# A transformer layer in split fp32: the first-stage modulation spread in eight pieces through the first head pair

## The chip, the cores and the metric

One Trainium2 chip, one core of it. The metric is the time of one execution on the device in microseconds (us), and the median over runs is what two kernels are compared by.

## What is computed

One layer of a diffusion-like transformer for 256 latent tokens `x`, with 256 context tokens `ctx` beside them, width 2048, 16 heads of 128:

```python
s_lat = silu(c); s_ctx = silu(c_ctx)                 # 2048 each
m_lat = split(s_lat @ w_ada + b_ada, 6)              # shift, scale, gate | shift, scale, gate
m_ctx = split(s_ctx @ w_ada + b_ada, 6)              # only shift and scale are used
a_lat = modulate(rms_norm(x, norm_mix), m_lat[0], m_lat[1])
a_ctx = modulate(rms_norm(ctx, norm_mix), m_ctx[0], m_ctx[1])
y = hgrn2_mixer(a_ctx, a_lat, ...)                   # w_in, w_f, gated linear scan per head, w_o
h = x + m_lat[2] * y
h = h + m_lat[5] * swiglu(modulate(rms_norm(h, norm_ffn), m_lat[3], m_lat[4]))
out = rms_norm(h, final_norm)
```

Everything is fp32. `w_ada` is 2048 x 12288 fp32; its first 4096 columns (shift and scale of the mixer, 32 MB) are needed for both token sets, the other 8192 for the latent tokens alone.

## The kernel before, in words

**Numbers.** TensorE multiplies in a rounded format (fp32r). Each weight chunk of 128 x 1024 floats is loaded into a ring of four slots (`raw`), ScalarE (ACT) writes its rounded part (`whi`, `hi`, L484) and VectorE (DVE) the rest (`wlo`, `lo`, L807), both in rings of three. Activations are split likewise into `ahi` and `alo`. A product is three matmuls. A matmul in plain fp32 is two records in the trace.

**Stage 1, the modulation.** 64 blocks of `w_ada` (128 rows x 1024 columns) are taken in four quarters of the columns, 16 blocks each. silu(c) and silu(c_ctx) stand in TensorE as four columns and the weights move, 512 columns at a time. 40 blocks are split (L1244, L1246), 24 go unsplit in fp32 through six slots of their own, `dslot` (L1236). The sums are four rows, which ACT copies (L502) and TensorE turns (L1256) before DVE makes `mod`, `modc` and `scl` of them. The 64 transposes of `x` and `ctx` (L1274) lie behind block 6, the matmul that spreads the mean squares (L1290) behind block 8. ACT modulates (L525), rounds (L528) and DVE makes the rest (L842).

**Stage 2, eight head pairs.** Each pair has 16 chunks: eight VQ (values and queries, 36 matmuls of 256 columns, the `v_bank` ones at L1310 to L1312) and then eight Z (both forget gates, 24 matmuls of 512 columns, L1295 to L1297). The scans of heads whose pairs are done run in steps between the chunks, by a table written by hand. DVE meanwhile adds up the other 96 blocks of `w_ada` (six sums that end by chunk 150, `ADA_ENDS`, one DVE operation of L903 for each block, then eight fp32 matmuls with one column, L1529).

**Stage 3, the output gate.** 32 chunks of `w_in`, here called the gate stage, with the scans of the last heads beside them.

**Stage 4 to 6.** Projection with `w_o` (32 chunks, `wide`, L1439 to L1441), FFN gate and up (176 chunks, L1419 to L1421), down (88 chunks, `wide` again). In the projection, SyncE (SP) asks for chunk 0, then waits for the last head's scan and asks for `x` by token, the gate row and the final weight (3.5 MB), then for chunk 1. ACT evacuates the last output gates (`gate_silu(3)`) before it splits chunk 1. The last three chunks of down run bank by bank (`wide_end`), so that the closing work can begin on the first bank.

The order on every engine is written by hand: each engine runs its own list in order, and semaphores tie the lists.

Of the kernel before, what the change touches and what calls it, by code (L numbers as in the profile page):

```python
# [19 lines left out]
F32 = mybir.dt.float32  # L20
# [30 lines left out]
def ada_direct(k):  # L51

    return k % 8 in (1, 4, 6)


SPLIT_ADA = [c for c in range(4 * KD) if not ada_direct(c % KD)]
DIRECT_ADA = [c for c in range(4 * KD) if ada_direct(c % KD)]
DIRECT = 6


def ada_column(q):

    return (2 * (1 - q % 2) + q // 2) * CW


X_AT = 6
C_B = len(SPLIT_ADA)
# [33 lines left out]
def positions():  # L101


    for g in range(GROUPS):
        for p in range(BODY):
            kind = "Z" if p % 16 >= 8 else "VQ"
            tasks = [(j, 4 * g + off) for j, off in tasks_at(p) if 4 * g + off >= 0]
            yield C_B + g * BODY + p, kind, 2 * g + p // 16, p % 8, tasks
    for p in range(32):
        yield C_G + p, "G", p // 8, p % 8, tasks_tail(p)  # L110


def build(nc, x, c, ctx, c_ctx, w_ada, b_ada, norm_mix, norm_ffn, lb_logits, w_in, w_f, o_norm, w_o,
# [4 lines left out]
    wada = w_ada[0].rearrange("(k p) n -> k p n", p=P)  # L118
    win = w_in[0].rearrange("(k p) n -> p k n", p=P)
# [6 lines left out]
    with stack:  # L126
# [61 lines left out]
        cs4 = sb("cs4", [P, KD, 2, 2], F32R)  # L188
        csd = sb("csd", [P, KD, 2, 2])
        xsum = sb("xsum", [P, 4])  # L190
        mod = sb("mod", [P, 6, KD])
        modc = sb("modc", [P, 2, KD])
        arow = aacc[0:4, :]
        scl = sb("scl", [P, 2, KD])
# [30 lines left out]
        s_c4 = sem("silu_c_split")  # L225
        s_ar = sem("mod_rows_ready")
        s_at = sem("mod_rows_turned")
# [9 lines left out]
        s_mod = sem("mod_steps")  # L237
# [81 lines left out]
        def _(sp):  # L319
# [19 lines left out]
            def load(ck):  # L339
# [3 lines left out]
                if ck < C_B:  # L343

                    q, k = divmod(SPLIT_ADA[ck], KD)
                    col = ada_column(q)
                    whole(slot, dst, wada[k, :, col:col + CW])
                elif ck < C_G:
                    pr, r = divmod(ck - C_B, 16)
                    kk = 2 * (r % 8)  # L350
# [22 lines left out]
            def load_direct(j):  # L373
                if j >= DIRECT:
                    sp.wait_ge(s_du, j - DIRECT + 1)
                q, k = divmod(DIRECT_ADA[j], KD)
                col = ada_column(q)
                sp.dma_start(dslot[j % DIRECT], wada[k, :, col:col + CW]).then_inc(s_dir[j % DIRECT], 16)

            for rb in range(4 * KD):  # L380
                if rb == 2:
                    sp.dma_start(brow[0:96, :], b_ada[0].rearrange("(k p) -> k p", p=P)).then_inc(s_vrow, 16)
                    sp.dma_start(vrow[R_ONORM:R_ONORM + 1, :], o_norm).then_inc(s_vrow, 16)
                if rb == X_AT:
                    for t in range(4):
                        sp.dma_start(xin[:, t, :], crows[t] if t < 2 else xrows[t - 2]).then_inc(s_x[t], 16)
                if ada_direct(rb % KD):
                    load_direct(DIRECT_ADA.index(rb))
                else:
                    load(SPLIT_ADA.index(rb))  # L390

# [16 lines left out]
            for ck in range(C_B, CHUNKS):  # L408
                load(ck)
                if ck == C_B + 4:  # L410
                    sp.dma_start(keep[:, :], keep_in).then_inc(s_keep, 16)
                    sp.dma_start(masks[:, :], masks_in).then_inc(s_keep, 16)
# [44 lines left out]
        def abank(q, i):  # L457

            return (score[0:4, i, :] if q % 2 == 0 else (bank[3], ob)[i][0:4, :])
# [18 lines left out]
        def _(act):  # L478
# [12 lines left out]
            for i in range(2):  # L491
                act.activation(cs[:, :, i], mx[:, 224 + i * KD:224 + (i + 1) * KD], ACT.Silu).then_inc(s_cs, 1)
            act.wait_ge(s_cs, 2)
            act.activation(cs4[:, :, :, 0], cs[:, :, :], ACT.Copy).then_inc(s_c4, 1)

            def mod_rows(q):

                act.wait_ge(s_used, C_B // 4 * (q + 1))
                if q:
                    act.wait_ge(s_at, q)  # L500
                for i in range(2):
                    act.activation(arow[:, i * 512:(i + 1) * 512], abank(q, i), ACT.Copy).then_inc(s_ar, 1)  # L502

            def x_rstd():

                for t in range(4):
# [12 lines left out]
            def modulate(k):  # L519

                act.wait_ge(s_mod, 6 if k < 8 else 11)
                act.wait_ge(s_xn, k + 1)
                for i in range(2):
                    v = xn[:, k, i * T:(i + 1) * T]
                    act.activation(v, v, ACT.Identity, bias=(modc, mod)[i][:, 0, k:k + 1],  # L525
                                   scale=scl[:, i, k:k + 1]).then_inc(s_am, 1)
# [3 lines left out]
            for rb in range(4 * KD):  # L530
                if rb == X_AT:
                    x_rstd()
                if not ada_direct(rb % KD):
                    hi(SPLIT_ADA.index(rb))
                if rb == 5:
                    act.preload_act_table_set(EXP_LN)
                if rb == 11:
                    act.wait_ge(s_lb, 1)
                    act.activation(lbt[:, 1, :], lbt[:, 0, :], ACT.Exp).then_inc(s_lb, 1)
                if rb == 10:  # L540
                    act.wait_ge(s_ms, 1)
                    act.activation(rstd[:, :], bank[2][:, :], ACT.Copy).then_inc(s_rs, 1)
                if rb % KD == 2 and rb > KD:
                    mod_rows(rb // KD - 1)
                if 40 <= rb < 56 and rb % 2 == 0:
                    modulate(rb // 2 - 20)
            hi(C_B)
            mod_rows(3)
            hi(C_B + 1)
            for k in range(8, KD):  # L550
                modulate(k)
                if k % 2 == 1:
                    hi(C_B + k // 2 - 2)
            for i in range(6, KD // 2 + 2):
                hi(C_B + i)

# [33 lines left out]
            def queries(pr):  # L590
                b = pr % 2
                act.wait_ge(s_used, C_B + 16 * pr + 8)
# [66 lines left out]
            for ck, kind, u, r, tasks in positions():  # L659
                if ck > C_B + KD // 2:  # L660
                    hi(ck + 1)
                if kind == "Z" and r == 0:
# [11 lines left out]
                if kind == "Z" and r == 0:  # L674
# [18 lines left out]
            for k in range(KD):  # L693
# [5 lines left out]
                else:  # L699
# [74 lines left out]
            for i in range(2 * KF):  # L774
# [5 lines left out]
                if i == 0:  # L780
# [23 lines left out]
        def _(dve):  # L804
# [6 lines left out]
            dve.memset(csd[:, :, :, 1], 0.0)  # L811
            dve.memset(eps[:, :], EPS).then_inc(s_one, 1)
            dve.wait_ge(s_cs, 2)
            dve.tensor_copy(csd[:, :, :, 0], cs[:, :, :]).then_inc(s_c4, 1)
            dve.wait_ge(s_c4, 2)
            dve.tensor_tensor(cs4[:, :, :, 1], cs[:, :, :], cs4[:, :, :, 0].bitcast(F32), ALU.subtract).then_inc(s_c4, 1)
            am = mx[:, 0:128].rearrange("p (m k s i) -> p m k s i", m=2, s=2, i=2)

            def modulation(q):


                m, half = 1 - q % 2, q // 2
                ks = slice(8 * half, 8 * half + 8)
                b = bias[:, m * KD + 8 * half:m * KD + 8 * half + 8]
                first = 2 + 5 * half + 3 * (q % 2)
                dve.wait_ge(s_at, q + 1)
                dve.tensor_tensor(mod[:, m, ks], am[:, q % 2, ks, 0, 0], b, ALU.add)
                dve.tensor_tensor(modc[:, m, ks], am[:, q % 2, ks, 1, 0], b, ALU.add).then_inc(s_mod, 1)
                dve.wait_ge(s_mod, first)
                dve.tensor_tensor(mod[:, m, ks], am[:, q % 2, ks, 0, 1], mod[:, m, ks], ALU.add)  # L830
                dve.tensor_tensor(modc[:, m, ks], am[:, q % 2, ks, 1, 1], modc[:, m, ks], ALU.add).then_inc(s_mod, 1)
                if m == 1:
                    dve.wait_ge(s_mod, first + 1)
                    nm = vec[:, R_NMIX + 8 * half:R_NMIX + 8 * half + 8]
                    dve.scalar_tensor_tensor(out=scl[:, 0, ks], in0=modc[:, 1, ks], scalar=1.0, in1=nm, op0=ALU.add,
                                             op1=ALU.mult)
                    dve.scalar_tensor_tensor(out=scl[:, 1, ks], in0=mod[:, 1, ks], scalar=1.0, in1=nm, op0=ALU.add,
                                             op1=ALU.mult).then_inc(s_mod, 1)
# [5 lines left out]
            for rb in range(4 * KD):  # L844
                if rb == X_AT:
                    dve.wait_ge(s_vecT, 1)
                    dve.tensor_copy(vec[:, :], mx[:, 0:VROWS]).then_inc(s_vec, 1)
# [815 lines left out]
```

## Time and profile before

| | |
|---|---|
| median of 3 runs | 1844.18 us (1842.5 to 1844.32) |
| the profiled execution | 1842.78 us, span in the trace 1841.0 us |
| TensorE (PE) busy | 1782.6 us, 97% |
| weight loads (PEld) busy | 1500.8 us, 82% |
| DVE busy | 1264.4 us, 69% |
| ACT busy | 899.4 us, 49% |
| chain that ended last | PE 84%, DVE 10%, issue 2%, ACT 2%, DMA 2% |
| mean granted TensorE clock | 0.992 |

The profile is one execution. Busy times of an engine are a union over its instructions; matmuls overlap, so the distance from one start to the next is what a matmul costs in a stream, not its own length. The chain of waits goes back from the last instruction to what released each. Stretches are given in us from the span's start: stage 1 is 0 to 112, the first pair 112 to 191, pairs two to eight 191 to 843, the gate stage 843 to 983, the projection 983 to 1086, gate and up to 1580, down to the end.

### The profile page before, as it was taken

To read this page: it belongs to the slowest core of one execution; us is meant where nothing else is said; L and a number is where in the kernel's file an instruction comes from. 1 tells how busy PE (TensorE), PEld (TensorE's weight loads), DVE (VectorE), ACT (ScalarE), POOL (GpSimd) and SP (SyncE) were. 2 spreads that over 40 slices of the span, in tenths; PEclk is the share of its full clock that TensorE was granted. 3 is DMA by queue.
4 is the path that set the end of the run, shared out by engine and by line. 5 is a ranking of instruction groups with operands and counts; after the bars stand their busy time and mean duration, and the time that the engine had idled before them with its cause. 6 is when DMAs were issued, how large, how long until landed. Compare 5 with 4: busy or idle time off the path is not lost.

```text
span 1841.0 us, 25084 instructions
## 1 busy us (share of the span) xinstructions
PE 1782.6 (97%) x9791; PEld 1500.8 (82%) x9791; DVE 1264.4 (69%) x1977; ACT 899.4 (49%) x1279; POOL 0.2 (0%) x4
## 2 busy tenths in 40 slices
PE   7999999999999999999888989999999999999997
PEld 2268989898989898988787878888888888788885
DVE  6763779796979796979975575555555555555755
ACT  6673535354545454545454554444444444455554
POOL 0000000000000000000000000000000000000000
PEclk9999999999999999999999999999999999999998
DMA  9974544554444554444656556777767776655553
GB/s 357 370 232 157 183 144 142 162 159 139 140 147 149 159 165 135 149 138 139 225 185 230 174 164 204 242 225 229 233 214 224 237 221 216 204 193 194 192 193 121
DMA packets 178136, 353.82 MB, mean 192 GB/s; under 512 B 16929, under 2 KB 82786, under 8 KB 176994
## 3 DMA queue, kind: packets, MB, share of 16 engines
q1 hardware_dynamic: 177826, 352.18, 59.4%
q8 instruction: 77, 1.26, 0.3%
q14 instruction: 41, 0.34, 0.1%
q10 hardware_dynamic: 192, 0.05, 0.0%
HBM read 350.06 MB, written 2.11 MB: 191 GB/s over the span
## 4 chain that ended last, share of the span: by engine, by line
PE 84%; DVE 10%; issue 2%; ACT 2%; DMA 2%; ACTq 0%; DVEq 0%
PE bank L1419 9%; PE bank L1421 9%; PE bank L1420 9%; PE bank L1295 8%; PE bank L1296 7%; PE bank L1297 7%; PE bank L1310 3%; PE bank L1439 3%; PE bank L1311 3%; PE bank L1440 3%; PE bank L1312 3%; PE bank L1441 3%; PE score L1499 2%; DVE wlo L807 2%; DVE aacc L903 2%
## 5 line engine op out<-in xcount | busy, mean ns | idle before, releaser
L807 DVE TENSOR_TENSOR wlo<-raw,whi 128x1024 fp32r<-128x1024 f32 x496 | 605.3, 1223 | 442.7 <-ACT whi L484 442.0
L484 ACT ACTIVATE whi<-raw 128x1024 fp32r<-128x1024 f32 x496 | 523.0, 1058 | 671.4 <-PE bank L1421 227.0
L1295 PE MATMUL bank<-ahi,whi 128*128 128x256 f32 (+1 forms) x1024 | 352.4, 344 | 10.8 <-DVE wlo L807 10.5
L1296 PE MATMUL bank<-alo,whi 128*128 128x256 f32 (+1 forms) x1024 | 344.8, 337 | 0.0
L1297 PE MATMUL bank<-ahi,wlo 128*128 128x256 f32 (+1 forms) x1024 | 344.7, 337 | 0.0
L1419 PE MATMUL bank<-whi,ahi 128*128 128x512 f32 x704 | 275.9, 392 | 1.8 <-DVE alo L1138 1.8
L1421 PE MATMUL bank<-whi,alo 128*128 128x512 f32 x704 | 274.5, 390 | 0.0
L1420 PE MATMUL bank<-wlo,ahi 128*128 128x512 f32 x704 | 274.4, 390 | 0.0
L1295 PEld LDWEIGHTS bank<-ahi,whi 128*128 128x128 f32 x1024 | 194.7, 190 | 32.2 <-DVE wlo L807 10.2
L1297 PEld LDWEIGHTS bank<-ahi,wlo 128*128 128x128 f32 x1024 | 194.7, 190 | 20.3
L1296 PEld LDWEIGHTS bank<-alo,whi 128*128 128x128 f32 x1024 | 194.9, 190 | 19.0
L1419 PEld LDWEIGHTS bank<-whi,ahi 128*128 128x128 f32 x704 | 132.6, 188 | 29.4 <-issue 2.2
L1421 PEld LDWEIGHTS bank<-whi,alo 128*128 128x128 f32 x704 | 132.4, 188 | 27.8
L1420 PEld LDWEIGHTS bank<-wlo,ahi 128*128 128x128 f32 x704 | 132.7, 188 | 27.1
L903 DVE SCALAR_TENSOR_TENSOR aacc<-raw,cs,aacc 128x1024 f32<-128x1024 f32 x120 | 153.5, 1279 | 0.5
L1310 PE MATMUL bank<-whi,ahi 128*128 128x256 f32 x512 | 147.3, 288 | 1.3 <-DVE arena L916 1.2
L1312 PE MATMUL bank<-whi,alo 128*128 128x256 f32 x512 | 144.8, 283 | 0.0
L1311 PE MATMUL bank<-wlo,ahi 128*128 128x256 f32 x512 | 144.7, 283 | 0.0
L1439 PE MATMUL bank<-whi,ahi 128*128 128x512 f32 x240 | 94.9, 396 | 8.9 <-DVE wlo L807 8.9
L1310 PEld LDWEIGHTS bank<-whi,ahi 128*128 128x128 f32 x512 | 98.1, 192 | 2.7 <-DVE wlo L807 2.5
L1311 PEld LDWEIGHTS bank<-wlo,ahi 128*128 128x128 f32 x512 | 98.1, 192 | 0.2
L1312 PEld LDWEIGHTS bank<-whi,alo 128*128 128x128 f32 x512 | 98.0, 191 | 0.0
(226 smaller groups left out, 2285.5 us busy)
## 6 DMA issues: line engine op xcount, KB each, us to landing
raw<-in_w_ada_dram SPq DMA_DIRECT2D x168, 512.0 KB, 3.9
raw<-in_ffn_w_gate_dram SPq DMA_DIRECT2D x88, 512.0 KB, 3.9
raw<-in_ffn_w_up_dram SPq DMA_DIRECT2D x88, 512.0 KB, 4.1
raw<-in_ffn_w_down_dram SPq DMA_DIRECT2D x88, 512.0 KB, 4.2
raw<-in_hg_w_in_dram SPq DMA_DIRECT2D x128, 256.0 KB, 3.4
raw<-in_hg_w_f_dram SPq DMA_DIRECT2D x128, 256.0 KB, 3.5
raw<-in_hg_w_in_dram SPq DMA_DIRECT2D x32, 512.0 KB, 4.6
raw<-in_hg_w_o_dram SPq DMA_DIRECT2D x32, 512.0 KB, 4.1
```

What stands on the lines that cost most here:

```text
L484: act.activation(whi[:, ck % SPL, :], raw[:, q % RAW, :], ACT.Copy).then_inc(s_hi, 1)
L807: dve.tensor_tensor(wlo[:, ck % SPL, :], raw[:, SEQ["w", ck] % RAW, :], whi[:, ck % SPL, :].bitcast(F32), ALU.subtract).then_inc(s_lo, 1)
L903: dve.scalar_tensor_tensor(out=aacc[:, :], in0=block, scalar=cs[:, k, 0:1], in1=aacc[:, :], op0=ALU.mult, op1=ALU.add).then_inc(s_ac, 1)
L1295: pe.matmul(dst, w, ah, start=start, stop=False, skip_group_check=True)
L1296: pe.matmul(dst, w, al, start=False, stop=False, skip_group_check=True)
L1297: return pe.matmul(dst, wl, ah, start=False, stop=stop, skip_group_check=True)
L1310: pe.matmul(dst, ahi[:, k, tk], whi[:, s, o], start=st, stop=False, skip_group_check=True)
L1311: pe.matmul(dst, ahi[:, k, tk], wlo[:, s, o], start=False, stop=False, skip_group_check=True)
L1312: last = pe.matmul(dst, alo[:, k, tk], whi[:, s, o], start=False, stop=end, skip_group_check=True)
L1419: pe.matmul(dst, ahi[:, k, tk], whi[:, s, o], start=first, stop=False)
L1420: pe.matmul(dst, ahi[:, k, tk], wlo[:, s, o], start=False, stop=False)
L1421: last = pe.matmul(dst, alo[:, k, tk], whi[:, s, o], start=False, stop=end)
```

## The change

- Stage 1 no longer stands ahead of the mixer. The 64 blocks are cut anew: eight pieces of 256 channels, eight blocks each, a block being 2 x 128 rows of 256 shift and 256 scale columns (two DMAs of 256 KB with 1 KB rows, `load_mod`). The weights stand in fp32, unsplit, and silu(c), silu(c_ctx) move as two columns: eight matmuls for each block (`mod_block`), through the six slots of `dslot`. The sums come out as columns, so nothing is copied and turned; one DVE pair (`modulation(e)`) gives shift and scale of a piece.
- Twelve blocks run ahead of chunk 0, the other 52 run four to a chunk between the parts of chunks 0 to 12. Chunks of the first pair alternate VQ, Z, and the first pair's Z sums lie in other banks.
- `x` and `ctx` are loaded first and turned ahead of the first block. The rows of vectors (`vrow`, `brow`) are turned before them.
- The ends of DVE's six sums move from (34, 54, 82, 102, 131, 150) to (22, 50, 70, 98, 118, 150).
- Projection: SP asks for chunks 0 to 4 before it waits for the last scan; ACT splits chunk 1 before `gate_silu(3)`. Down: `turn_hidden` and what surrounds it lie behind chunk 1, not 0; `wide_end` takes two chunks, not three; the closing DVE operations are in another order.

```diff
-            for rb in range(4 * KD):
-                if rb == 2:
-                    sp.dma_start(brow[0:96, :], b_ada[0].rearrange("(k p) -> k p", p=P)).then_inc(s_vrow, 16)
...
+            def load_mod(n):
+
+                if n >= DIRECT:
+                    sp.wait_ge(s_du, n - DIRECT + 1)
+                e, j = divmod(n, 8)
+                for m in range(2):
+                    sp.dma_start(dslot[n % DIRECT][:, m * 512:(m + 1) * 512].rearrange("p (k n) -> p k n", k=2),
+                                 wmod[:, 2 * j:2 * j + 2, m * D + e * 256:m * D + (e + 1) * 256]).then_inc(s_dir[n % DIRECT], 16)
+
+            for t in range(4):
+                sp.dma_start(xin[:, t, :], crows[t] if t < 2 else xrows[t - 2]).then_inc(s_x[t], 16)
+            sp.dma_start(brow[0:96, :], b_ada[0].rearrange("(k p) -> k p", p=P)).then_inc(s_vrow, 16)
+            sp.dma_start(vrow[R_ONORM:R_ONORM + 1, :], o_norm).then_inc(s_vrow, 16)
+            for n in range(8):
+                load_mod(n)
...
             for ck in range(C_B, CHUNKS):
+                if ck == 1:
+                    for n in range(8, FIRST):
+                        load_mod(n)
+                elif ck >= 2:
+                    for n in mod_blocks(ck - 2):
+                        load_mod(n)
                 load(ck)
...
-                if ck == C_WO:
+                if ck == C_WO + 4:
 
                     sp.wait_ge(s_on, HEADS)
...
+        def mod_block(pe, n):
+
+            e, j = divmod(n, 8)
+            pe.wait_ge(s_dir[n % DIRECT], 32 * (n // DIRECT + 1))
+            if n == 0:
+                pe.wait_ge(s_cs, 2)
+            if j == 0 and e >= 2:
+                pe.wait_ge(s_md, 2 * e - 1)
+            w = dslot[n % DIRECT].rearrange("p (s k n) -> p s k n", k=2, s=2)
+            for k in range(2):
+                for i in range(4):
+                    last = pe.matmul(mod_sums(e)[:, 2 * i:2 * i + 2], w[:, i // 2, k, i % 2 * P:(i % 2 + 1) * P], cs[:, 2 * j + k, :],
+                                     start=(n in (0, 8) and k == 0 and i == 0), stop=(j == 7 and k == 1), skip_group_check=True)
+            last.then_inc(s_du, 1)
...
+            pe.wait_ge(s_vrow, 16 * 6)
+            pe.transpose(score[:, 1, 0:VROWS], vrow[0:VROWS, :], ident[0:VROWS, 0:VROWS])
...
+            for i in range(KD):
+                turn_x(i)
+            for n in range(FIRST):
+                mod_block(pe, n)
+                if n == 3:
...
+                    if u == 0 and i < 4:
+                        for n in mod_blocks(ck)[i:i + 1]:
+                            mod_block(pe, n)
...
-            wide_end([(C_DN + i, i % YR) for i in range(2 * KF - 3, 2 * KF)], s_db)
-
-
-ADA_ENDS = (34, 54, 82, 102, 131, 150)
+            wide_end([(C_DN + i, i % YR) for i in range(2 * KF - 2, 2 * KF)], s_db)
+
+
+ADA_ENDS = (22, 50, 70, 98, 118, 150)
```

PE at the start of the program, as it was: `mx` and `score` are sums, `cs` and `csd` silu(c) standing, `work` and `arena` hold `dslot` and `x`.

```order
L1264 MATMUL mx<-ident,crow 128x32
L1244 MATMUL score<-whi,cs 4x512
L1246 MATMUL score<-wlo,cs 4x512
...
L1236 MATMUL score<-work,csd 4x512 x2
...
L1281 MATMUL mx<-ident,arena 128x65
L1282 MATMUL mx<-ident,arena 128x96
L1274 MATMUL bank<-ident,arena 128x128 x64
```

PE at the same place in the changed kernel, up to the first part of chunk 0 (L1189 is `mod_block`, 8 rows to a block; `ob` and `mx` its sums; L1242 to L1244 `v_bank`):

```order
L1198 MATMUL score<-ident,crow 128x32
L1200 MATMUL score<-ident,arena 128x65
L1201 MATMUL score<-ident,arena 128x96
L1211 MATMUL bank<-ident,arena 128x128 x64
L1189 MATMUL ob<-cs,work 128x2 x24
L1189 MATMUL ob<-cs,arena 128x2 x8
L1222 MATMUL bank<-zt,ones 128x512
L1189 MATMUL ob<-cs,arena 128x2 x16
L1189 MATMUL ob<-cs,work 128x2 x16
L1189 MATMUL mx<-cs,work 128x2 x8
L1189 MATMUL mx<-cs,arena 128x2 x24
L1242 MATMUL bank<-whi,ahi 128x256
```

The transposes of the vectors and of `x` now head the list, and twelve blocks of eight follow before the first chunk.

SP at the start of the projection, as it was and then as it is (`work<-in_x_dram` is `x` by token):

```order
L324 DMA raw<-in_hg_w_o_dram 128x1024
L421 DMA work<-in_x_dram 128x2048 x2
L401 DMA work<-gate_rows 128x2048
L405 DMA arena<-in_final_norm_dram 128x1024
L324 DMA raw<-in_hg_w_o_dram 128x1024 x31
```

```order
L315 DMA raw<-in_hg_w_o_dram 128x1024 x5
L412 DMA work<-in_x_dram 128x2048 x2
L386 DMA work<-gate_rows 128x2048
L390 DMA arena<-in_final_norm_dram 128x1024
L315 DMA raw<-in_hg_w_o_dram 128x1024 x27
```

Four more chunks are asked for ahead of the 3.5 MB.

## Rows read from the trace of the kernel before

**Rows 1.** The page, part 1: busy us, share of the span, instructions

```profile
PE 1782.6 (97%) x9791; PEld 1500.8 (82%) x9791; DVE 1264.4 (69%) x1977; ACT 899.4 (49%) x1279; POOL 0.2 (0%) x4
```

**Rows 2.** Busy time by stretch: us; PE, PEld, DVE, ACT, POOL; PE clock; DMA share; GB/s

```profile
0.00:112.00 112.00, 98.60 (x349) 26.79 (x350) 76.74 (x109) 70.83 (x92) 0.20 (x4) 1.00 0.95 354
...
191.00:843.00 652.00, 650.49 (x4256) 594.81 (x4255) 546.98 (x1067) 321.57 (x506) 0.00 (x0) 1.00 0.48 149
...
870.00:930.00 60.00, 47.34 (x365) 45.70 (x364) 59.10 (x115) 27.73 (x38) 0.00 (x0) 0.94 0.63 200
```

**Rows 3.** PE by time, start and us: first VQ, first Z, second pair

```profile
112.08 0.28 PE L1310 MATMUL bank<-whi,ahi 128*128 128x256 f32 x1
...
147.68 0.40 PE L1295 MATMUL bank<-ahi,whi 128*128 128x512 f32 x1
...
191.23 0.28 PE L1310 MATMUL bank<-whi,ahi 128*128 128x256 f32 x1
```

**Rows 4.** DMA issues of 0 to 14 us: KB each, median us to landing

```profile
arena<-in_x_dram SPq DMA_DIRECT2D x2, 1024.0 KB, 15.1
```

**Rows 5.** The chain of waits, opening: start, us, what

```profile
10.27 3.51 PE score L1236 x4
...
19.52 9.66 DVE work L852 x16
...
32.59 0.87 PE bank L1290 x2
```

**Rows 6.** PE by time around the first sum of L1529 (fp32 standing)

```profile
287.52 1.84 PE L1529 MATMUL bank<-ones,aacc 128*128 128x1 f32 x16
289.23 0.36 PE L1310 MATMUL bank<-whi,ahi 128*128 128x256 f32 x1
289.43 0.28 PE L1311 MATMUL bank<-wlo,ahi 128*128 128x256 f32 x1
```

**Rows 7.** PE by time: eight transposes of the modulation rows, 4 columns each

```profile
114.31 0.65 PE L1256 MATMUL mx<-ident,aacc 4*128 4x4 f32 x8
```

**Rows 8.** PE by time: fp32 of 128 columns at half clock

```profile
927.27 0.63 PE L1512 MATMUL ob<-work 128*128 128x128 f32 x2
927.69 0.64 PE L1513 MATMUL ob<-work 128*128 128x128 f32 x2
```

**Rows 9.** DVE groups, gate stage (843 to 983): busy us, mean ns

```profile
L903 DVE SCALAR_TENSOR_TENSOR aacc<-raw,cs,aacc 128x1024 f32<-128x1024 f32 x16 | 20.5, 1279 | 0.0
```

**Rows 10.** Busy time by stretch, two at half clock (columns as in rows 2)

```profile
922.50:929.30 6.80, 5.18 (x25) 5.19 (x25) 6.80 (x13) 4.04 (x4) 0.00 (x0) 0.50 0.57 166
990.70:994.10 3.40, 3.33 (x8) 2.69 (x9) 3.20 (x5) 1.51 (x3) 0.00 (x0) 0.50 0.59 177
```

**Rows 11.** PE by time, start of the projection

```profile
985.24 0.39 PE L1441 MATMUL bank<-whi,alo 128*128 128x512 f32 x1
990.77 0.77 PE L1439 MATMUL bank<-whi,ahi 128*128 128x512 f32 x1 [5.14 <-DVE wlo L807]
```

**Rows 12.** The chain of waits there: start, us, what

```profile
976.39 11.89 DMA raw<-in_hg_w_o_dram
```

**Rows 13.** PE by time: down behind its chunk 0, and its last three chunks

```profile
1587.17 0.47 PE L1439 MATMUL bank<-whi,ahi 128*128 128x512 f32 x1 [3.77 <-DVE wlo L807]
...
1817.11 0.39 PE L1441 MATMUL ob<-whi,alo 128*128 128x512 f32 x1
1820.05 0.69 PE L1439 MATMUL score<-whi,ahi 128*128 128x512 f32 x1 [2.56 <-DVE wlo L807]
```

**Rows 14.** DVE by time, one closing operation of 128x512

```profile
1824.70 0.69 DVE L1097 TENSOR_TENSOR work<-zt,work 128x512 f32<-128x512 f32 x1
```

**Rows 15.** PE by time: the transposes of x and the fp32 matmuls behind them

```profile
18.89 8.62 PE L1274 MATMUL bank<-ident,arena 128*128 128x128 f32 x64
27.43 1.88 PE L1236 MATMUL score<-work,csd 128*4 128x512 f32 x4
```

**Rows 16.** The page, part 6: KB each, median us from issue to landing

```profile
raw<-in_w_ada_dram SPq DMA_DIRECT2D x168, 512.0 KB, 3.9
```

More of the change, by code:

```diff
@@ L48, with mod_blocks @@
 BODY = 32
[L51 to L57, printed above, removed]
 DIRECT = 6
[L61 to L67, printed above, removed]
+FIRST = 12
+C_B = 0
+def mod_blocks(ck):
+    return list(range(FIRST + 4 * ck, min(FIRST + 4 * ck + 4, 64)))
 C_G = C_B + GROUPS * BODY
@@ L491, in _ @@
             for i in range(2):
[L492 to L502, printed above, removed]
+                act.activation(cs[:, :, i], score[:, 0, i * KD:(i + 1) * KD], ACT.Silu).then_inc(s_cs, 1)
+            act.preload_act_table_set(EXP_LN)
             def x_rstd():
+                act.wait_ge(s_one, 1)
                 for t in range(4):
@@ L524, in modulate @@
                     v = xn[:, k, i * T:(i + 1) * T]
-                    act.activation(v, v, ACT.Identity, bias=(modc, mod)[i][:, 0, k:k + 1],
-                                   scale=scl[:, i, k:k + 1]).then_inc(s_am, 1)
+                    act.activation(v, v, ACT.Identity, bias=modx[:, k, 0, 1 - i:2 - i],
+                                   scale=scl[:, k, 1 - i:2 - i]).then_inc(s_am, 1)
                 act.wait_ge(s_am, 2 * (k + 1))
                 act.activation(ahi[:, k, :], xn[:, k, :], ACT.Copy).then_inc(s_ah, 1)
[L530 to L555, printed above, removed]
+            x_rstd()
+            act.wait_ge(s_lb, 1)
+            act.activation(lbt[:, 1, :], lbt[:, 0, :], ACT.Exp).then_inc(s_lb, 1)
+            act.wait_ge(s_ms, 1)
+            act.activation(rstd[:, :], bank[2][:, :], ACT.Copy).then_inc(s_rs, 1)
+            modulate(0)
+            modulate(1)
+            hi(0)
             UNITS = ((0, 0), (1, 0), (0, 1), (1, 1))
@@ L1302, in v_bank @@
                 first, end = k == 0, k == KD - 1
-                if first and u:
+                if first and u == 1:
+                    pe.wait_ge(s_vev, half + 1)
+                elif first and u:
                     pe.wait_ge(s_zc, 4 * (u - 1) + 1 + 2 * half)
@@ L1380, in chunk_z @@
                         last.then_inc(s_zd, 1)
+                    if u == 0 and i >= 3:
+                        for n in mod_blocks(ck)[i - 3:i - 2]:
+                            mod_block(pe, n)
                 last.then_inc(s_used, 1)
@@ L1577, in _ @@
                          {0: (s_fh, 2 * FG - 1), 1: (s_fh, 2 * FG), 2: (s_av, 8)})
-                for k in range(KF - 3 * half):
+                for k in range(KF - 2 * half):
                     i = KF * half + k
```

280 lines of the change are left out of this document (104 added, 176 removed).

## The prediction

> **What bounds the kernel now.** I read the page's busy times first, then the busy times by stretch, the chain of waits, and TensorE's instructions by time wherever two stages meet. PE is busy 97% of the span [rows 1], so only two things can move the end: what PE has to do, and the few places where it stands still. The stretches tell them apart [rows 2]. Until 112 us the DMA share is 0.95 at 354 GB/s: 32 MB of shift and scale weights and 4 MB of tokens come in, and PE works on 64 blocks in their shadow. From 191 to 843 us PE is busy for 650.5 of 652 us, DMA share 0.48: bound by PE alone. From 870 to 930 us PE has 47.3 of 60 us while DVE has 59.1: this stretch is DVE's. So the change moves 52 of 64 blocks out of a stretch bound by DMA into one bound by PE. That can pay only if a block costs PE less there than the DMA time it frees.
>
> **The first projection starts earlier.** Today chunk 0 starts at 112.08 us and the second pair at 191.23, 79.15 us later [rows 3]. In the changed kernel PE's list is: turn c, turn the vectors, turn x, twelve blocks, chunk 0. The vector transposes wait for `brow`, which SP asks for behind the four 1 MB tiles. A DMA lands behind what its queue was asked for before it: a tile of x takes 15.1 us today, behind the blocks ahead of it [rows 4]. So nothing is turned before 4.3 MB are in: 4.3 MB at 354 GB/s [rows 2] are 12.1 us, with some 3 us for the first issue and the last landing that is 15 us (estimate). The 64 transposes take 9.66 us, paced by DVE's copies [rows 5], hence 24.7 us. Then come the blocks.
>
> **What a block costs PE.** The trace has the same form, with one moving column, not two: eight fp32 matmuls with 128x128 standing, 16 records, start at 287.52; the next matmul starts at 289.23, 1.71 us later, and the one behind it another 0.20 us on, where the stream has 0.12 between two of 256 columns [rows 3, 6]. So 1.71 us among its like, and 1.71 + 0.08 = 1.79 between other matmuls. One column more is nothing beside 107 ns for a record. Bounds: from below 0.65 us for eight small transposes with a weight load each [rows 7], so at most 81 ns for a record and 1.3 us for 16; from above 0.425 us for two records at half clock [rows 8], 3.4 us a block. I take 1.71 and 1.79, the nearest row. DMA does not hold it back: 0.52 MB in 1.71 us are 307 GB/s in the opening, under the 354 of [rows 2], and far less later, when chunks lie between.
>
> Twelve blocks and the mean-square matmul (0.87 us, [rows 5]) are 21.4 us, so chunk 0 starts at 46.1 us. Behind block 7 ACT and DVE modulate two k, split them and chunk 0: about 7 us that lie beside blocks 8 to 11 (6.8 us) and cost nothing here, up to 2 us if ACT is late. From there to the second pair the work of today's stretch runs (79.15 us, less 0.6 for the last turned rows, [rows 3, 7]) plus 52 blocks x 1.79 = 93.1 us: 171.7 us. The second pair starts at 217.8 instead of 191.23: **26.5 us later**. What goes away, 40 blocks' splitting on ACT and DVE, was hidden behind DMA and gives nothing. In a word: the blocks cost PE 64 x 1.7 = 109 us, as much as the 112 us they replace, and the tokens' transposes now stand open ahead of them.
>
> **What comes back later.**
> - Gate stage. From chunk 132 to 148 sixteen accumulations run, one to a chunk, 1.28 us of DVE each [rows 9], where DVE is full [rows 2]. PE's idle time there is 60 - 47.3 = 12.7 us, and 6.8 us run at half clock, 3.4 us lost [rows 10]. The new ends spread the last sum from chunk 119 on, which leaves nine accumulations in the same chunks, one to every second: 7 x 1.28 = **9.0 us less**. Bounds: nothing (the waits move to the scan's DVE steps) and 16 us (all of both). The earlier sums become denser in places, where DVE has 105 us to spare over 652 [rows 2]: zero, as long as no eight chunks get more than eight.
> - Projection. PE stands from 985.47 to 990.77, 5.3 us, and then runs 3.4 us at half clock, 1.7 us more [rows 10, 11]. The chain gives the reason, chunk 1's DMA of 11.89 us behind 3.5 MB [rows 12]. It is now asked for first, and ACT splits it before `gate_silu(3)`. The late one next is chunk 5; it lands some 10 us after the 3.5 MB are asked for, five chunks of 2.72 us (12 x 0.227, the distance of 192 such matmuls between 147.68 and 191.23, [rows 3]) in: in time. **7.0 us less.**
> - Down, behind its first chunks: PE waits 3.8 us behind the transposes for a chunk split only after `hidden_back` [rows 13]. The change moves transposes, evacuation and the split behind them together by one chunk. Same order, same wait: nothing.
> - Down, last chunks: the wait of 2.7 us [rows 13] for the last of three splits goes, since the third chunk from the end runs meanwhile, and with it 1.7 us of half clock. The last banks then come 1.4 us apart, not 2.0, while DVE needs three operations of 0.69 us for each [rows 14], so its closing work queues: I give back 0.7. **3.7 us less.**
>
> Sum: 26.5 - 9.0 - 7.0 - 3.7 = **+6.8 us**. Against the profiled execution's 1842.8 this is 1849.6; the median of the runs lies 1.4 above it, so I say **1851.0**. About 0.2% (3.7 us) is what a measurement here tells from no change.
>
> **A rule weighed.** The transposes of the opening run at full clock today: four records of fp32 matmuls with 512 columns behind 8.6 us of nothing but transposes take 1.88 us, four alike at 10.27 us took 3.51 [rows 15, 5]. The clock was high when they ended. The Trainium skill, page "TensorE: Matmul & The Clock Gate", section "Part 4: PE-mode transpose", says that the full clock does not come with transposes, as they do not count as PE being busy. By that rule the changed opening, which has transposes alone, would reach its blocks at half clock, and the time would be the 1871 of the second rival; by the row it would not. I go by the row in the sum and keep the other as a rival.
>
> **Rivals.**
> - *The blocks hide partly, and DVE's relief is full* (ends faster or level). PE takes weight loads ahead of running matmuls, so a block between two dense parts might lose less than 1.79 us. With 1.6 us that is 10 us less, with the gate stage's upper bound 5 more: 1836. It decides once 3.1 us of my sum go (then within 0.2%), and is faster than before by more than that once 10.5 go. Against it: the 1.79 was measured in just such a place, between dense matmuls. Chance 0.20, half of it over 0.2% on the fast side of today, with the fast end of my own range beside it.
> - *Half clock in the opening.* PE ran at 0.50 after it had stood still, as in [rows 10]; blocks of two moving columns may not hold the clock up, and the transposes before them may not raise it. Twelve blocks at 3.4 instead of 1.7 us: +20.5, 1871. For: nothing in the trace shows full clock over a long stretch of such matmuls, only 1.7 us at a time. Against: [rows 15]. Chance 0.13.
> - *Half clock through the first pair.* The same, where blocks take most of PE's time between dense parts: 52 x 1.7 = 88 us for blocks, up to 63 us more for the dense parts of chunks 0 to 12 (seven VQ of 4.3 and six Z of 5.4 us, [rows 3]) and the opening's 20: 1940 to 2020. Chance 0.10. A granted clock of 0.5 between 50 and 200 us would show it.
> - *The change does not do what it says*: blocks starve, since each of the six slots is asked for again only when its block is done. The next six blocks leave it 8 us or more, a DMA of 512 KB lands in 3.9 [rows 16]. Chance 0.05, a few us.
>
> **How the numbers follow.** Forecast 0.52, with its own range 1840 to 1861: ±4 for the opening, ±5 for the gate stage, ±3 for the seams. The whole range must take in the half clock of the opening and the block's lower price: 1834 to 1875, which leaves out the first pair at half clock and the far ends. Faster by over 0.2%: 0.20, from the first rival and the fast end of the forecast. Within: 0.16. Slower: 0.64.
>
> **What would show it.** Chunk 0 near 46 us and the second pair near 218; `mod_block` groups of 16 records every 1.7 us; granted clock 1.00 from 20 to 218 us; PE without a wait behind the projection's chunk 0; PE idle from 870 on (shifted by 27) down by 9 us; the wait behind down's transposes unchanged. A second pair before 205 us would say that a block costs less than this row; one after 235, that the clock fell.

## The result, and the profile after

The changed kernel takes **1977.51 us** (median of 4 runs, 1972.08 to 1985.41) against 1843.96 for the kernel before (4 runs): a ratio of 1.0733 [1.0712, 1.0753], 7.3% slower. The profiled execution took 1972.08 us, its span is 1970.3, 129.3 longer than before. The prediction said 1851.0, with 1834 to 1875 as its range.

The page, parts 1 and 2, of the changed kernel (to be read beside [rows 1]):

```profile
PE 1916.5 (97%) x10527; PEld 1700.1 (86%) x10527; DVE 1217.0 (62%) x1930; ACT 853.5 (43%) x1230; POOL 0.2 (0%) x4
...
PE   7999999999999999999988999999999999999997
...
PEclk7565658999999999999999999999999999999999
```

The last of these rows in the kernel before:

```profile
PEclk9999999999999999999999999999999999999998
```

PE is busy 97% of the span, as before; little keeps it waiting. But in the row PEclk the second to sixth slices (49 us each) stand at 5 and 6 tenths and the first and seventh at 7 and 8, where the kernel before has 9 (90% or more). The clock itself was granted at two levels only, 0.50 and 1.00 (1.2 and 2.4 GHz); a figure between them is the mean of a stretch. Busy time by stretch gives each stage its share: first of the changed kernel, cut at the start of the blocks, chunk 0, the second pair, the gate stage, the projection, and gate and up; columns as in [rows 2].

```profile
24.78:63.84 39.06, 39.06 (x197) 38.03 (x195) 11.23 (x22) 5.82 (x9) 0.00 (x0) 0.55 0.60 187
63.84:327.20 263.36, 263.36 (x1313) 251.31 (x1314) 45.07 (x60) 40.26 (x61) 0.00 (x0) 0.63 0.46 147
327.20:984.52 657.32, 653.95 (x4271) 598.06 (x4270) 552.88 (x1077) 323.75 (x509) 0.00 (x0) 1.00 0.50 153
984.52:1122.02 137.50, 121.16 (x979) 118.23 (x978) 114.41 (x218) 77.36 (x120) 0.00 (x0) 0.99 0.53 163
1122.02:1219.41 97.39, 92.36 (x421) 75.43 (x419) 56.15 (x71) 50.80 (x79) 0.00 (x0) 1.00 0.63 210
1219.41:1970.30 750.89, 736.57 (x3288) 610.22 (x3288) 428.52 (x467) 342.74 (x435) 0.00 (x0) 0.99 0.67 209
```

The same view of the kernel before for its gate stage, its projection and what follows (its other stretches are in [rows 2, 3]):

```profile
843.16:982.72 139.56, 123.33 (x995) 120.80 (x994) 119.71 (x225) 76.08 (x118) 0.00 (x0) 0.98 0.60 193
982.72:1086.57 103.85, 93.91 (x421) 76.58 (x419) 57.74 (x73) 52.26 (x81) 0.00 (x0) 0.98 0.58 190
1086.57:1841.00 754.43, 737.18 (x3288) 610.59 (x3288) 428.70 (x467) 342.84 (x435) 0.00 (x0) 0.99 0.65 208
```

The account of the 129.3 us, beside what was predicted:

| Stretch | before | after | difference | predicted |
|---|---|---|---|---|
| start to second pair | 191.23 | 327.20 | +136.0 | +26.5 |
| seven further pairs | 651.9 | 657.3 | +5.4 | 0 |
| gate stage | 139.6 | 137.5 | -2.1 | -9.0 |
| projection | 103.9 | 97.4 | -6.5 | -7.0 |
| gate, up, down | 754.4 | 750.9 | -3.5 | -3.7 |

So it is the front. PE by time in the changed kernel, first where the blocks begin, then a piece of the first pair:

```profile
24.78 6.77 PE L1189 MATMUL ob<-cs,work 128*128 128x2 f32 x48
31.41 3.55 PE L1189 MATMUL ob<-cs,arena 128*128 128x2 f32 x16
...
97.08 0.77 PE L1225 MATMUL ob<-ahi,whi 128*128 128x512 f32 x1
97.66 0.63 PE L1226 MATMUL ob<-alo,whi 128*128 128x512 f32 x1
98.08 0.63 PE L1227 MATMUL ob<-ahi,wlo 128*128 128x512 f32 x1
98.51 3.41 PE L1189 MATMUL mx<-cs,work 128*128 128x2 f32 x16
101.78 0.77 PE L1225 MATMUL ob<-ahi,whi 128*128 128x512 f32 x1
```

The first three blocks take 6.63 us, and the clock falls on the way, at 28.6 us; from there on one block takes 3.4 us, twice the 1.71 of [rows 6]. The chunk's own matmuls beside it take 0.43 us from start to start instead of 0.23: the low clock is paid by everything in that stretch, not by the blocks alone. (The clock comes back for 3 to 7 us at a time in the pair, which gives the mean of 0.63.) Down to the start of the blocks the working held: the vector transposes began at 15.01 us (predicted 15) and the 64 transposes of x ended at 24.9 (predicted 24.7).

### The profile page after: what moved, and what is told of

It reads as the page before. It is cut to its first block, busy times and chain, and to the rows that moved or that the text cites. A ratio compares the mean times of both kernels' runs of the same rounds, so it can differ in the third digit from the quotient of the medians.

```text
span 1970.3 us, 26516 instructions
## 1 busy us (share of the span) xinstructions
PE 1916.5 (97%) x10527; PEld 1700.1 (86%) x10527; DVE 1217.0 (62%) x1930; ACT 853.5 (43%) x1230; POOL 0.2 (0%) x4
## 4 chain that ended last, share of the span: by engine, by line
PE 88%; DVE 6%; ACT 2%; issue 2%; DMA 1%; SPq 0%; ACTq 0%; DVEq 0%
PE bank L1357 8%; PE bank L1359 8%; PE bank L1358 8%; PE mx L1189 8%; PE bank L1225 7%; PE bank L1226 7%; PE bank L1227 7%; PE bank L1242 3%; PE bank L1243 3%; PE bank L1244 3%; PE bank L1377 3%; PE bank L1378 3%; PE bank L1379 3%; PE score L1439 2%; PE score L1377 1%
## 5 line engine op out<-in xcount | busy, mean ns | idle before, releaser
L777 DVE TENSOR_TENSOR wlo<-raw,whi 128x1024 fp32r<-128x1024 f32 x456 | 556.5, 1223 | 387.7 <-ACT whi L479 387.4
L479 ACT ACTIVATE whi<-raw 128x1024 fp32r<-128x1024 f32 x456 | 480.4, 1058 | 604.6 <-PE bank L1359 223.3
L1225 PE MATMUL bank<-ahi,whi 128*128 128x256 f32 (+1 forms) x976 | 340.7, 349 | 7.9 <-DVE wlo L777 7.7
L1226 PE MATMUL bank<-alo,whi 128*128 128x256 f32 (+1 forms) x976 | 330.8, 339 | 0.0
L1227 PE MATMUL bank<-ahi,wlo 128*128 128x256 f32 (+1 forms) x976 | 330.4, 339 | 0.0
L1357 PE MATMUL bank<-whi,ahi 128*128 128x512 f32 x704 | 275.7, 392 | 1.8 <-DVE alo L1091 1.8
L1226 PEld LDWEIGHTS bank<-alo,whi 128*128 128x128 f32 x976 | 190.3, 195 | 16.7
L1242 PE MATMUL bank<-whi,ahi 128*128 128x256 f32 x512 | 157.6, 308 | 3.1 <-DVE wlo L777 1.9
L1357 PEld LDWEIGHTS bank<-whi,ahi 128*128 128x128 f32 x704 | 132.6, 188 | 29.3 <-issue 2.2
L1359 PEld LDWEIGHTS bank<-whi,alo 128*128 128x128 f32 x704 | 132.5, 188 | 27.8
L1244 PE MATMUL bank<-whi,alo 128*128 128x256 f32 x512 | 152.7, 298 | 0.0
L512 ACT ACTIVATE arena<-arena,modx,scl 128x256 f32<-128x256 f32 x32 | 17.4, 590 | 230.7 <-DVE scl L795 230.7
L1242 PEld LDWEIGHTS bank<-whi,ahi 128*128 128x128 f32 x512 | 106.4, 208 | 5.3 <-DVE wlo L777 4.5
```

The costliest lines, as they stand in the source:

```text
L479: act.activation(whi[:, ck % SPL, :], raw[:, q % RAW, :], ACT.Copy).then_inc(s_hi, 1)
L777: dve.tensor_tensor(wlo[:, ck % SPL, :], raw[:, SEQ["w", ck] % RAW, :], whi[:, ck % SPL, :].bitcast(F32), ALU.subtract).then_inc(s_lo, 1)
L1225: pe.matmul(dst, w, ah, start=start, stop=False, skip_group_check=True)
L1226: pe.matmul(dst, w, al, start=False, stop=False, skip_group_check=True)
L1227: return pe.matmul(dst, wl, ah, start=False, stop=stop, skip_group_check=True)
L1242: pe.matmul(dst, ahi[:, k, tk], whi[:, s, o], start=st, stop=False, skip_group_check=True)
```

## Experiments

**Is it the clock, and what lowers it?** My theory after the result: what PE did while the granted clock stood at 0.5 was mostly these blocks, which load 128x128 and move two columns, and the same blocks moving more columns would run at 1.00. The rival: a block is slow by its weight loads, whatever moves. Two kernels tell them apart. In the first, each of a block's matmuls moves silu(c)'s two columns 32 times over (a stride of zero), into 64 columns of the bank, of which the first two are read (so the pieces behind the first now share one place for their sums):

```diff
+WIDE = 64
-            return (ob if e == 0 else mx)[:, 8 * e:8 * e + 8]
+            return (ob if e == 0 else mx)[:, 0:4 * WIDE].rearrange("p (c w) -> p c w", c=4)
...
+                return bass.AP(tensor=c.tensor, offset=c.offset, ap=[list(c.ap[0]), [0, WIDE // 2], [1, 2]])
...
-                    last = pe.matmul(mod_sums(e)[:, 2 * i:2 * i + 2], w[...], cs[:, 2 * j + k, :],
+                    last = pe.matmul(mod_sums(e)[:, i, :], w[...], moving(k),
```

> The changed kernel, with silu(c) moving as 64 columns (the same two, repeated by a stride of zero) instead of 2 in all 64 blocks. The same 16 records to a block, the same weights standing, the same result. Theory A (TensorE's granted clock falls while matmuls that move two columns take most of its time, although its busy share stays at 100%): the clock stays at 1.0 from some 20 us on, a block takes 1.7 to 1.8 us, the second pair starts at 218 to 225 us instead of 327, and the time is 1865 to 1875. Rival B (a block costs 3.3 us among its like, whatever moves, because loading 128x128 of fp32 weights again and again is what lowers the clock): clock 0.62 from 64 to 325 us as before, time 1970 to 1985. Rival C (moved columns cost by themselves): clock 1.0, but blocks of over 2.5 us, time above 1900.

Measured: 1868.58 us (1863.23 to 1872.61), 109 us less than the changed kernel, ratio to the kernel before 1.0127 [1.0104, 1.0149]. Busy time by stretch (start of the blocks, chunk 0, second pair, then the half clock inside the pair) and two blocks by time:

```profile
24.23:46.45 22.22, 22.22 (x197) 21.74 (x195) 9.73 (x20) 5.83 (x9) 0.00 (x0) 1.00 0.83 266
46.45:227.48 181.03, 179.73 (x1314) 171.21 (x1314) 46.64 (x63) 40.34 (x61) 0.00 (x0) 0.95 0.70 221
195.30:212.40 17.10, 17.10 (x81) 17.00 (x80) 1.02 (x3) 2.65 (x5) 0.00 (x0) 0.50 0.28 101
```

```profile
95.44 1.89 PE L1195 MATMUL mx<-cs,arena 128*128 128x64 f32 x16
97.15 0.36 PE L1231 MATMUL bank<-ahi,whi 128*128 128x256 f32 x1
...
97.94 1.90 PE L1195 MATMUL mx<-cs,arena 128*128 128x64 f32 x16
99.64 0.36 PE L1248 MATMUL bank<-whi,ahi 128*128 128x256 f32 x1
```

Theory A holds. The same 16 records and the same weight loads, with 32 times the columns, take 1.71 us to the next matmul: the added columns cost no time (that they hide behind the weight loads is my reading), and the clock stays at 1.00 from the blocks' start up to 195 us. Chunk 0 starts at 46.45, where the prediction had 46.1; the second pair starts at 227.5, a little later than expected, of which more below.

The second kernel puts such blocks into six later pairs of the kernel before, a different dose in each:

```diff
+            DOSE = {1: (4, 2), 2: (2, 2), 3: (1, 2), 4: (4, 16), 5: (4, 64), 6: (4, 96)}
+                for j in range(8):
+                    pe.matmul(bank[f][:, 0:width], whi[:, ck % SPL, j * P:(j + 1) * P].bitcast(F32),
+                              ahi[:, k, 0:width].bitcast(F32), start=False, stop=False, skip_group_check=True)
```

> The kernel before, with added fp32 matmuls between the chunks' parts in the pairs 1 to 6 (twelve of the sixteen chunks of each), of eight matmuls with 128x128 standing (the chunk's own weights) that add to a live bank, so the output is wrong by those sums. Pair 1: 4 blocks to a chunk, 2 columns moving; pair 2: 2 blocks, 2 columns; pair 3: 1 block, 2 columns; pair 4: 4 blocks, 16 columns; pair 5: 4 blocks, 64 columns; pair 6: 4 blocks, 96 columns. Pair 1 is 85.1 us long today, the others 92.9 to 95.5; at full clock 48 blocks add 48 x 1.79 = 86 us, 24 add 43, 12 add 21. Theory A (moved columns hold the clock): pair 1 at a clock of some 0.6 and 150 to 175 us longer, pair 3 at 1.0 and 21 longer, pair 2 between, pair 4 nearer to pair 1, pairs 5 and 6 at 1.0 and 86 to 95 longer. Rival B (fp32 weight loads lower the clock): pairs 1, 4, 5 and 6 all at about 0.6 and 150 us or more longer.

Measured in one execution (2406.03 us). Busy time by stretch, one row for each dosed pair:

```profile
189.41:436.73 247.32, 247.32 (x1312) 234.88 (x1311) 68.13 (x118) 41.40 (x56) 0.00 (x0) 0.67 0.18 56
436.73:594.90 158.17, 158.17 (x1010) 149.31 (x1009) 83.61 (x161) 47.18 (x75) 0.00 (x0) 0.86 0.32 97
594.90:711.10 116.20, 116.20 (x818) 108.26 (x817) 79.59 (x158) 46.93 (x75) 0.00 (x0) 1.00 0.37 117
711.10:948.83 237.73, 237.73 (x1378) 225.14 (x1377) 79.50 (x156) 46.92 (x75) 0.00 (x0) 0.73 0.18 57
948.83:1134.16 185.33, 185.33 (x1394) 177.14 (x1393) 83.68 (x161) 46.96 (x75) 0.00 (x0) 0.97 0.27 83
1134.16:1314.65 180.49, 180.49 (x1394) 172.50 (x1393) 80.19 (x158) 46.96 (x75) 0.00 (x0) 1.00 0.24 77
```

| Pair | blocks, columns | without blocks | with | per block | clock |
|---|---|---|---|---|---|
| 1 | 48, 2 | 85.1 | 247.3 | 3.38 | 0.67 |
| 2 | 24, 2 | 95.1 | 158.2 | 2.63 | 0.86 |
| 3 | 12, 2 | 95.5 | 116.2 | 1.72 | 1.00 |
| 4 | 48, 16 | 92.9 | 237.7 | 3.02 | 0.73 |
| 5 | 48, 64 | 95.1 | 185.3 | 1.88 | 0.97 |
| 6 | 48, 96 | 95.5 | 180.5 | 1.77 | 1.00 |

("Without" is the same pair of the kernel before, from the same view; per block is the difference divided by their number.) Each pair lies where theory A put it, to within a microsecond; the rival is refuted by pairs 5 and 6. At one block to a chunk the two-column form costs 1.72 us, almost exactly the price that I took: the price was right for the density at which it was measured, and doubles at the density at which it was to be paid. But 64 columns do not hold the clock everywhere. Pair 5 starts at full clock and loses it inside, for 10 us, with no wait of PE ahead of it: four blocks' matmuls among a chunk's, then the 16 records of one of DVE's sums, which move one column, stand right behind a block's.

```profile
970.83 1.90 PE L1356 MATMUL bank<-ahi,whi 128*128 128x64 f32 x16
972.56 2.00 PE L1541 MATMUL bank<-ones,aacc 128*128 128x1 f32 x16
```

```profile
974.30:984.30 10.00, 10.00 (x49) 10.00 (x48) 1.93 (x3) 2.15 (x4) 0.00 (x0) 0.50 0.18 52
```

Whether that sum brought the fall was not tried; pair 6, with 96 columns, stays at 1.00.

**What is left of the blocks' price without their records?** The changed kernel with one matmul of eight in 46 of the 52 blocks of the pair:

```diff
                 for i in range(4):
+                    if n >= FIRST and j and (k, i) != (1, 3):
+                        continue
```

> The changed kernel, with one matmul of eight in 46 of the 52 blocks that lie between the first pair's chunks (the first block of each eighth is whole); shift and scale are wrong by that. Transfers and order stay. Theory A (with blocks rare the clock stays at 1.0 there): after the opening (chunk 0 at 63.8) the pair takes 79.15 + 6 x 1.79 + 46 x 0.3 = 104 us, so the second pair starts at 167 instead of 327: 160 us for 46 x 7/8 = 40 blocks, 4.0 us each, of which 1.8 are their own and the rest is what their clock costs them and the chunks. Rival B (the chunks of the first pair run slowly for another reason, such as DVE and ACT preparing tokens between them): the clock stays near 0.6 and the pair takes over 150 us.

Measured: 1829.46 us in one run. Busy time by stretch, the first pair:

```profile
63.26:184.24 120.98, 111.42 (x669) 100.01 (x670) 45.45 (x60) 41.10 (x61) 0.00 (x0) 0.93 0.99 318
```

The pair takes 121.0 us instead of 263.4, so 40 blocks' worth of records cost 142 us, 3.6 each; expected were 4.0 and a pair of 104. The row tells where the 17 us between come from: DMA share 0.99. With the blocks' PE work gone, their 27 MB bound the pair; PE is idle for 9.6 us (the longest waits, for blocks' transfers, are 2.5 us before 140.3 and 3.3 before 160.6), and some 7 us at half clock follow each of the two. Theory A holds on the clock, with a mean of 0.93. An estimate comes with it: 121 less the 79 us of the pair before, so in this order of transfers the 52 blocks could hardly have been had for less than some 40 us, whatever they cost PE.

**What kept the 64-column kernel 10 us behind my sum?** Its first pair takes 181.0 us where the prediction had 171.7, with 17.1 us at half clock at its end. The waits of SP's own queue between 170 and 212 us, first group:

```profile
SPq L344 <- DVE aacc L845: 9.3, 1, 9.3
```

SP stands 9.3 us for the slot of an accumulation's block (`load_ada`), and the requests for shift and scale blocks are behind it; PE then waits 1.3 us for one, and the clock falls at 195.3. The edit starts those accumulations three chunks later:

```diff
-    begin = ADA_ENDS[e - 1] + 1 if e else 10
+    begin = ADA_ENDS[e - 1] + 1 if e else 13
```

> The kernel with 64 moving columns, and the accumulations of the first other factor begun at chunk 13 instead of 10 (two to a chunk in places). In the run with 64 columns SP waited 9.3 us for the slot of such an accumulation, with the requests for shift and scale blocks behind it in its queue; PE then waited 1.3 us for a block's transfer at 191.7 us and ran at a clock of 0.5 from 195.3 to 212.4. Theory A (that queue is the cause): no half clock before 218 us, second pair 9 to 10 us earlier (227.3 -> 218), time 1857 to 1861. Rival B (blocks are slow to land by DMA's own load there, or the clock falls by PE's own work): the half clock stays, time 1865 to 1872.

Measured: 1869.58 us (1866.89 to 1871.15), no change. Busy time by stretch, the first and the second pair, and behind it the second pair of the run before:

```profile
46.78:219.72 172.94, 171.60 (x1314) 163.45 (x1314) 42.87 (x60) 40.02 (x60) 0.00 (x0) 1.00 0.69 221
219.72:315.82 96.10, 89.77 (x559) 80.95 (x558) 77.10 (x131) 44.02 (x60) 0.00 (x0) 0.98 0.59 187
```

```profile
227.48:317.77 90.29, 87.69 (x559) 79.27 (x558) 73.14 (x128) 43.84 (x59) 0.00 (x0) 1.00 0.57 179
```

In this trace the half clock is gone and the first pair takes 172.9 us (predicted 171.7), as theory A has it. The time was not 1857 to 1861: the accumulations now fall two to a chunk, into the second pair too, whose PE waits for DVE's splitting up to 230.5, 237.3, 242.4 and 249.4 (0.5 to 2.4 us each), and which is 5.8 us longer; of the 8 us won 2 are left, less than the medians of 4 runs can tell.

That the queue was the cause isn't shown, though. The profiled execution of the 64-column kernel was the longest of its four (1872.61, mean clock 0.989). Another took 1863.23 at a mean clock of 0.996, which leaves room for some 15 us at half clock in the whole kernel: it cannot have had the 17 us stretch, and had the same order of transfers. So the edit may have removed what comes and goes by itself, and pair 5 above lost the clock at 64 columns without any wait. What is shown: 17.1 us at half clock (8.5 us lost) and the wait of 1.3 us make up the 10 us, and the edit lengthened the second pair.

**Do the seams stand on their own?** The kernel before with only the edits at the projection and at down (the diff is theirs in the change):

> The kernel before, with only the edits at the projection (order of SP's transfers, splitting of chunk 1 ahead of the gate's work) and at down (turned rows one chunk later, two chunks at the end instead of three, order of the last operations). In the changed kernel the projection was 6.5 us shorter and the end from down on 3.5 us. Theory A (these parts are independent of the front): 1844 - 10 = 1834, gap of 5.1 us behind the projection's first chunk gone, no gap at 1817. Rival B (the gaps went because the stages ahead ended at another moment relative to DMA): a gap stays and the time is 1839 to 1844.

Measured: 1833.49 us (1831.58 to 1834.3), ratio 0.9944 [0.9931, 0.9956]. Busy time by stretch, the projection:

```profile
983.00:1079.83 96.83, 92.02 (x419) 75.44 (x418) 56.29 (x71) 50.98 (x79) 0.00 (x0) 1.00 0.62 211
```

96.8 us where the kernel before has 103.9. In down's last chunks PE no longer waits either (2.56 us, up to 1820.05, before). Theory A: both seams are independent of the front, and worth 10.9 us. This is the best version of the study: it beats both kernels, the one before by 0.6%.

**Why did the gate stage not get shorter?** The kernel before with only the new `ADA_ENDS`:

> The kernel before, with only the table of the chunks at which each sum of the other factors ends (22, 50, 70, 98, 118, 150 instead of 34, 54, 82, 102, 131, 150), so that fewer accumulations of DVE lie in the gate stage. Theory A (the prediction's step: accumulations hold the scan up there): PE's idle time from 843 to 983 us falls from some 16 us to 8, time 1835. Theory B (the chain of the scan over DVE, ACT and PE sets the stage, and taking other work from DVE leaves its waits where they are): idle time 15 to 17 us and the time 1841 to 1845.

Measured: 1841.41 us (1839.16 to 1843.74), 0.9986 [0.9978, 0.9995]. And the kernel before with the stage's accumulations cut to 8 columns:

```diff
+                if e < 6 and ada_chunk(i) >= C_G:
...
+                    dve.scalar_tensor_tensor(out=aacc[:, 0:8], in0=block[:, 0:8], scalar=cs[:, k, 0:1],
+                                             in1=aacc[:, 0:8], op0=ALU.mult, op1=ALU.add).then_inc(s_ac, 1)
```

> The kernel before, with the accumulations of the other factors that lie in the gate stage (17 from 843 to 983 us, 1.28 us each) cut to 8 of 1024 columns; the fourth and fifth factors are wrong by that. Their transfers, waits and order stay. Theory A (the prediction's step, its upper bound): the stage loses 9 to 16 us, time 1828 to 1835. Theory B (the scan's chain sets the stage): it loses 0 to 4 us though DVE has 21 us less to do, time 1840 to 1844.

Measured: 1836.11 us (1832.85 to 1837.53), 0.9962 [0.9949, 0.9974]. The gate stage by stretch, first with the new ends, then with the small sums:

```profile
843.58:982.27 138.69, 122.32 (x979) 119.25 (x978) 112.95 (x216) 76.00 (x118) 0.00 (x0) 0.98 0.53 167
```

```profile
842.17:976.27 134.10, 122.19 (x996) 119.92 (x995) 103.05 (x225) 76.11 (x118) 0.00 (x0) 0.99 0.62 201
```

With the new ends DVE has 6.8 us less to do and PE's idle time is 16.4 us instead of 16.2; the stage is 0.9 us shorter, all of it PE's own work: a sum with its 16 records was moved out. With the small sums DVE has 16.7 us less and the stage loses 5.5: 4.3 of idle time, and 1.1 of busy time, with a half clock of 3.4 us instead of 6.8 (which the seams' run has too, with this stage unedited, so it need not come from the sums). PE still waits there: 1.6 us for `wlo` up to 893.9, 4.0 us for ACT's `rstd` up to 926.3. Two waits side by side show how they move:

```profile
924.12 0.58 PE L1295 MATMUL bank<-ahi,whi 128*128 128x256 f32 x1 [3.67 <-DVE wlo L807]
934.07 0.70 PE L1517 MATMUL mx<-rstd,ones 128*128 128x256 f32 x2 [1.70 <-ACT rstd L639]
```

```profile
916.41 0.39 PE L1301 MATMUL bank<-ahi,whi 128*128 128x256 f32 x1 [0.94 <-DVE wlo L807]
926.30 0.70 PE L1523 MATMUL mx<-rstd,ones 128*128 128x256 f32 x2 [3.98 <-ACT rstd L639]
```

First the kernel before, then the small sums: 2.7 us less for DVE's splitting, 2.3 more for the scan's `rstd`. So even the whole of DVE's extra work is worth 5.5 us, not 16, and less accumulation moves PE's wait from one step to the next. Theory B is borne out for the table; with the small sums the stage lost more than its 4 us and less than theory A's 9, and the time, too, lies between the two. Over the whole kernel the medians differ by 7.3 us, the two profiled executions by 9.9. Of these 9.9, 5.5 are the stage, 1.0 lies ahead of it and 3.5 behind it, in code that is the same in both: there the kernel before ran 3.4 us at half clock behind each of its two waits in down, and this execution, with the same waits, did not. It was the fastest of its five (1832.85; the others 1835.64 to 1837.53).

**Both together.** The kernel before with the seams and the ends:

> The kernel before with both the edits of the seams and the new table of ends. If they add: 1833.5 - 2.9 = 1830.6 us, 0.75% under the kernel before. If the table's 2.9 us came from the projection's gap, which the seams already close: 1833 to 1835.

Measured: 1833.91 us (1833.14 to 1835.0), 0.9953 [0.9939, 0.9966]. The table adds nothing to the seams. Whether its 2.9 us came from the projection's gap, as the second expectation has it, isn't shown: alone it left that gap at 5.0 us.

## Why the prediction was wrong, step by step

- **The opening, up to the blocks: right.** 15.0 and 24.9 us against 15 and 24.7. The transposes did bring the full clock: the record of the granted clock begins with 1.00 at 18.3 us, 3 us into them, and their pace tells that it was lower before: fourteen transposes in the 2.97 us ahead of that are 0.21 us each, fifty-two in the 6.64 us behind it 0.13 each. [rows 15] had shown only that transposes keep a clock that other matmuls had raised (ahead of them, at 15.99 us, four records of `csd` matmuls already took 1.88 us); that they raise it is new. I went by [rows 15] and not by the rule of the Trainium skill, page "TensorE: Matmul & The Clock Gate", section "Part 4: PE-mode transpose", that they do not count; the trace doesn't agree with that rule here.
- **"What a block costs PE": the step that failed.** "So 1.71 us among its like, and 1.71 + 0.08 = 1.79 between other matmuls ... I take 1.71 and 1.79, the nearest row." The row was a single block among dense matmuls, at full clock, and pair 3 of the doses confirms it (1.72). I had the upper bound in the same paragraph, 3.4 us a block at half clock, and named the condition in a rival ("blocks of two moving columns may not hold the clock up"), but put it at 0.13 for the opening and 0.10 for the pair, although I had written myself that "nothing in the trace shows full clock over a long stretch of such matmuls". The third rival is what happened: "A granted clock of 0.5 between 50 and 200 us would show it", and the clock there is 0.58 in the mean, over the whole pair 0.63. Its 1940 to 2020 holds the 1977.5. In place of 1.79, a two-column block cost 3.38 us at four to a chunk (pair 1 of the doses, with what the chunks lost by the clock). The second pair starts at 327.2 instead of 217.8: of these 109.4 us, 17.7 came in the opening (chunk 0 at 63.84 instead of 46.1) and 91.7 in the pair. With the clock at 1.00 by 64 columns, everything else of that sum comes out: 46.45 and, in the execution without a half clock in the pair, 172.9 us.
- **Where the range failed.** It was cut off at the opening's half clock (1871). But the opening and the pair run the same blocks, and in the pair four of them (6.8 us at full clock) go with one chunk of 4.3 to 5.4. If the clock is low beside them in the first place, nothing in the trace says that it isn't in the second; the two rivals were one, and its size was the larger.
- **"zero, as long as no eight chunks get more than eight", for the further pairs: off by 5.4 us.** The condition isn't met by the change itself: with the first end at 22, `ada_chunk` puts 12 of the first sum's 16 accumulations into chunks 10 to 17 (with the old end at 34 it was 6). Of the 5.4 us, 1.7 are the sum that was moved out of the gate stage; the rest is in the second pair, a wait of 1.87 us for DVE at 337.85 and 3.4 us at half clock behind it. The 64-column kernel has the same wait. Which of DVE's moved operations makes it late was not tried; but the kernel with all 16 in chunks 13 to 20 has four such waits in that pair.
- **Gate stage, -9.0: wrong.** The step "7 x 1.28 us less" counted DVE's work as PE's wait. The stage lost 2.1 us, all of it PE's busy time (121.2 instead of 123.3), and the moved sum, 1.7 us, accounts for most of that; PE's idle time stayed at 16.3. The lower bound of that term, "the waits move to the scan's DVE steps", was the answer.
- **Projection, -7.0: right** (-6.5; the gap behind chunk 0 is gone, no chunk behind it is late). **Down, -3.7: right** (-3.5 from gate and up to the end); the wait behind the turned rows stayed at 3.77 us, as predicted.

## What to carry to other kernels

A price for an instruction holds at the clock of the stretch it was read in. Before moving many small-column matmuls into a dense stretch, ask what the granted clock does when they are most of PE's time; here PE's busy share was 100% at 0.63 as at 1.00 and did not tell. Where a matmul's time does not depend on its moved columns, as between 2 and 64 here, moving more costs nothing and may keep the clock up, which gave 109 us back with a few lines. When a profile shows a stretch at half clock, look at the mean clock of the other executions before explaining it. And compare both currencies of a move: a block cost 1.7 us of PE in a PE-bound pair and freed 1.5 us of DMA (0.52 MB at 354 GB/s), so by this estimate the move could not have paid even at full clock, and the 64-column kernel, 1.3% slower than the one before, bears that out.

## What was new about the hardware

- Between chunks, blocks of fp32 matmuls with 128x128 standing and 2 columns moving ran at a mean granted clock of 0.67 with four to a chunk, 0.86 with two and 1.00 with one. With 16 columns it was 0.73 (four to a chunk), with 64 and 96 columns 0.97 and 1.00; the 0.97 is one fall of 10 us, without a wait ahead of it. PE was busy 100% of the time in each case, the weight loads 93 to 96%.
- Up to 64 columns the 16 records of a block take the same 1.71 us to the next matmul as with one column. At half clock it is 3.4 us with two columns. That the 128x128 weight load, which all of them share, sets this pace is inferred.
- In the opening PE had done next to nothing until the transposes of x began at 15.3 us, and behind these alone the granted clock stood at 1.00 from 18.3 us on; one transpose took 0.21 us before that and 0.13 after.
